# Dots, residual adds and tokens in another order: a transformer layer with 16,384 retrieved experts

## The reference, cut to what matters

```
x = LayerNorm(alpha * x + concat(diff_attention, stick_attention) @ w_out)      # "LN1"
q = x @ w_q                         # 8 heads, two halves of 128 each
s1, s2 = q . subkeys                # two times 128 scores a head
top 16 of s1, top 16 of s2, top 16 of the 256 sums  ->  16 experts a head, gates = softmax
act = gelu(x . peer_u[expert]) * gate
y = LayerNorm(alpha * x + sum act * peer_v[expert])                             # "LN2"
```

## Time and profile before

| | us |
|---|---|
| median of 3 runs | 2603.69 (2603.02 to 2605.6) |
| the profiled execution | 2600.89 |
| its span, first to last instruction | 2599.2 |
| PE busy | 2306.4 (89%) |
| DVE busy | 1468.4 (56%) |
| POOL busy | 678.5 (26%) |
| ACT busy | 377.4 (15%) |
| DMA 41%, PE 34%, DVE 14% | shares of the chain that ended last |

### The profile page before, as it was taken

One profiled execution on the slowest core, in us unless ns is written; L12 is line 12 of the kernel. 1 busy time (PEld: TensorE's weight loads), 2 busy tenths in 40 slices (PEclk: granted clock), 3 DMA queues, 4 the chain that ended last, 5 costly groups with the idle time before them and its releaser, 6 DMA issues.

```text
span 2599.2 us, 29221 instructions
## 1 busy us (share of the span) xinstructions
PE 2306.4 (89%) x11802; PEld 1677.5 (65%) x11802; DVE 1468.4 (56%) x2342; ACT 377.4 (15%) x657; POOL 678.5 (26%) x470
## 2 busy tenths in 40 slices
PE   8999999988965498887497999999999999999990
PEld 8999999947622388886487999644444444444440
DVE  3333333353578978776785760255555555555568
ACT  3333333321000211000032320000000000000001
POOL 2000000000254534221401010143334443443452
PEclk9999999999987699999799999999999999999995
DMA  6434444365999799999989988999999999999994
GB/s 251 142 141 145 141 141 144 144 262 219 405 391 397 295 421 376 417 421 421 396 290 365 361 320 318 343 415 413 418 418 418 408 421 414 417 416 420 417 394 200
DMA packets 129924, 861.41 MB, mean 331 GB/s; under 512 B 14752, under 2 KB 14880, under 8 KB 33824
## 3 DMA queue, kind: packets, MB, share of 16 engines
q1 hardware_dynamic: 63360, 425.88, 41.9%
q0 software_dynamic: 56960, 408.97, 38.7%
q10 hardware_dynamic: 9504, 25.17, 2.5%
HBM read 833.75 MB, written 26.21 MB: 331 GB/s over the span
## 4 chain that ended last, share of the span: by engine, by line
DMA 41%; PE 34%; DVE 14%; issue 5%; POOL 4%; ACT 1%; DVEq 0%; SPq 0%; ACTq 0%; POOLq 0%
DMA scratch<-peer_v,idx_v 26%; DMA arena<-peer_u,idx_u 13%; PE bank L1250 9%; DVE scratch L1642 5%; PE bank L970 4%; PE bank L971 3%; PE bank L974 3%; PE bank L1233 3%; POOL arena L576 2%; PE bank L1092 2%; DVE arena L1581 2%; PE bank L992 2%; PE bank L988 2%; PE bank L989 2%; DMA cache<-u_tiles 2%
## 5 line engine op out<-in xcount | busy, mean ns | idle before, releaser
L1581 DVE CUSTOM_DVE_ANT_0 arena<-arena,x 128x2048 f32<-128x2048 f32 x256 | 583.1, 2287 | 171.5 <-DMA arena<-peer_u,idx_u 171.2
L576 POOL DMA_INDIRECT arena<-peer_u,idx_u x256 | 358.0, 1398 | 650.2 <-DVE dots L1581 601.6
L1642 DVE SCALAR_TENSOR_TENSOR scratch<-scratch,gate 128x2048 f32<-128x2048 f32 x112 | 263.3, 2351 | 378.7 <-DMA scratch<-peer_v,idx_v 378.0
L591 POOL DMA_INDIRECT scratch<-peer_v,idx_v x112 | 251.8, 2249 | 462.9 <-DVE scratch L1642 444.7
L1250 PE MATMUL bank<-scratch,cache 128*128 128x128 f32 x2048 | 242.3, 278 | 40.1 <-DMA cache<-u_tiles 40.1
L1293 DVE TENSOR_TENSOR arena_rounded<-arena,w_high 128x1024 fp32r<-128x1024 f32 x96 | 113.9, 1224 | 266.5 <-ACT w_high L658 266.5
L1250 PEld LDWEIGHTS bank<-scratch,cache 128*128 128x128 f32 x2048 | 235.8, 194 | 44.4 <-DMA cache<-u_tiles 44.4
L1250 PE MATMUL bank<-scratch,ln_rows 128*128 128x128 f32 x2048 | 239.1, 276 | 26.2 <-DMA ln_rows<-u_tiles 22.6
L1250 PEld LDWEIGHTS bank<-scratch,ln_rows 128*128 128x128 f32 x2048 | 232.6, 192 | 30.5 <-DMA ln_rows<-u_tiles 28.4
L1270 PE MATMUL bank<-ln_rows,scratch 128*128 128x512 f32 x512 | 230.3, 592 | 0.7 <-ACT scratch L837 0.7
L1270 PE MATMUL bank<-cache,scratch 128*128 128x512 f32 x512 | 230.2, 592 | 0.0
(11 more groups left out here) (209 smaller groups left out, 2843.4 us busy)
## 6 DMA issues: line engine op xcount, KB each, us to landing
ln_rows<-u_tiles SPq DMA_DIRECT2D x64, 1024.0 KB, 8.9
cache<-u_tiles SPq DMA_DIRECT2D x64, 1024.0 KB, 10.0
ln_rows<-peer_v SPq DMA_DIRECT2D x64, 1024.0 KB, 10.0
cache<-peer_v SPq DMA_DIRECT2D x64, 1024.0 KB, 9.1
arena<-w_heads SPq DMA_DIRECT2D x32, 1024.0 KB, 5.0
arena<-w_out SPq DMA_DIRECT2D x24, 1024.0 KB, 8.3
arena<-w_heads SPq DMA_DIRECT2D x8, 2048.0 KB, 8.6
arena<-w_q SPq DMA_DIRECT2D x16, 1024.0 KB, 9.0
```

The source lines that it names most:

```text
L576: pool.indirect_dma_start(out=u_row[k % U_SLOTS], out_offset=None, in_=peer_u, in_offset=bass.IndirectOffsetOnAxis(ap=idx_u[:, p % 2, k:k ...
L591: pool.indirect_dma_start(out=v_row[slot], out_offset=None, in_=peer_v, in_offset=bass.IndirectOffsetOnAxis(ap=idx_v[:, q % 2, k:k + 1], a ...
L1581: dve.tensor_tensor_reduce(u_row[slot], u_row[slot], x1[:, 0 if p < H else 2, :], 1.0, 0.0, ALU.mult, ALU.add, dots[:, p % 2, k:k + 1]).th ...
L1642: dve.scalar_tensor_tensor(out=residual2, in0=v_row[slot], scalar=coef[:, GROUPS_DENSE + q, k:k + 1], in1=residual2, op0=ALU.mult, op1=ALU ...
```

## The change

- `add_residual(1, 0..3)` and LN1 of blocks 1 and 2 stand among 2, 2, 3, 3, 2, 2, 2 dots of group 1, instead of behind groups 1 and 2 and most of 3. `dots_and_choice(2, 0, 2)` and group 3 follow LN1.
- The choices of blocks 1 and 2 take groups 5, 6, 7; the last, `choose(1, 3)`, has no dots in it, and an explicit `weigh(7)` follows. Group 8, the first of block 2, moves into the tokens.
- Tokens begin at tiles 70 and 94 instead of 54 and 78. One dot stands ahead of every 16 tokens and six between, as before: they are dots 128 to 149 instead of 144 to 165.
- `TOGETHER` is 176 instead of 168: the dots left after the tokens are 150 to 175 (26) instead of 166 and 167; 80 instead of 88 dots remain for the second half.
- Key scores of block 0 get buffers of their own for pieces 1 and 2, so `copy_keys` waits only for piece 3. ACT's list is reordered to match: `copies(3)` ahead of the second exponents, LN1's scaling ahead of gelu 1, the third exponents and gelu 2 and 3 among the queries, gelu 8 and 9 in or after the tokens.

```diff
-TOGETHER = H * K + 40
+TOGETHER = H * K + 48
-HOT_AT = (54, 78)
+HOT_AT = (70, 94)
...
-        key_scores = [[cache[:, 3, :].rearrange("p (c l k) -> p c l k", c=2, l=LANES)] * 4,
-                      [flat[:, 3 * ROW + j * 1024:3 * ROW + (j + 1) * 1024]
-                       .rearrange("p (c l k) -> p c l k", c=2, l=LANES) for j in range(4)]]
+        after = [flat[:, 3 * ROW + j * 1024:3 * ROW + (j + 1) * 1024].rearrange("p (c l k) -> p c l k", c=2, l=LANES)
+                 for j in range(6)]
+        old_keys = cache[:, 3, :].rearrange("p (c l k) -> p c l k", c=2, l=LANES)
+        key_scores = [[old_keys, after[0], after[1], old_keys], after[2:6]]
...
# ACT
-                if grp == 0:
-                    act.wait_ge(half_read[grp], j + LEAD)
+                if grp == 0 and j == 3:
+                    act.wait_ge(half_read[grp], 1 + LEAD)
...
-            for i in range(2):
-                copy_query(0, 3, i)
+            copies(3)
             gate_numerators(0, 1)
...
             activate(0)
-            activate(1)
-            for i in range(2):
-                copy_keys(0, 3, i)
-            gate_numerators(0, 2)
-            activate(2)
             ln1_deviation(1)
             ln1_scale(1)
             copy_x1T(1)
+            activate(1)
...
-            activate(3)
...
+            gate_numerators(0, 2)
             queries(0)
+            activate(2)
             queries(1)
+            activate(3)
+            queries(2)
+            queries(3)
             gate_numerators(0, 3)
             activate(4)
-            queries(2)
-            queries(3)
-            dense = 0
-            for j, upto in enumerate((2, 6, 10, HOT_AT[0] // A_CHUNK)):
+            for c in range(4):
+                activate_dense(c)
+            dense = 4
+            for j, upto in enumerate((8, 12, 15, HOT_AT[0] // A_CHUNK)):
                 gate_numerators(1, j)
-                activate(5 + j)
+                if j < 3:
+                    activate(5 + j)
...
+                if t == HOT_AT[1] + P // HOT_PER_TILE + 4:
+                    activate(H + 1)
...
-                            activate(TOGETHER // K - 1)
+                            activate(H)
...
-            active = TOGETHER // K
+            active = H + 2
...
# DVE
-                if k == 3 and p > 0:
+                if k == 3 and p not in (0, H):
                     weigh(p - 1)
...
             dots_and_choice(0, 0, 1)
-            dots_of(1, 0, 8)
+            dots_of(1, 0, 2)
             add_residual(1, 0, out_banks(0), 4)
-            dots_of(1, 8, 16)
+            dots_of(1, 2, 4)
             add_residual(1, 1, out_banks(1), 2 * 4)
-            dots_and_choice(2, 0, 2)
+            dots_of(1, 4, 7)
             add_residual(1, 2, out_banks(2), 3 * 4)
+            dots_of(1, 7, 10)
             add_residual(1, 3, out_banks(3), 4 * 4)
             ln1_moments(1)
-            dots_of(3, 0, 2)
+            dots_of(1, 10, 12)
             ln1_shift(1)
-            dots_of(3, 2, 6)
+            dots_of(1, 12, 14)
             ln1_affine(1, 0)
-            dots_of(3, 6, 10)
             ln1_affine(1, 1)
-            dots_of(3, 10, 16)
+            dots_of(1, 14, 16)
+            dots_and_choice(2, 0, 2)
+            dots_of(3)
             dots_and_choice(4, 0, 3)
-            for j in range(4):
+            for j in range(3):
                 dots_and_choice(5 + j, 1, j)
-            i = (H + 1) * K
+            choose(1, 3)
+            weigh(H - 1)
+            i = H * K
```

## The result

The change makes the kernel faster, by less than half of what was forecast: 2588.8 us (median of four runs, 2587.9 to 2591.0) against 2604.6 us for the kernel before (median of four), ratio 0.9936 [0.9925, 0.9948]. That is 15.8 us less, where 34.9 were forecast (2569 us); 2588.8 lies in the range given. The profiled execution has a span of 2586.9 us, 12.3 less than before.

A forecast was written before the change was run, and what follows sets the result against it. No single bound: PE, DMA or DVE by stretch, so load time in the holes was counted. 10.8 (first token) + 13.8 (after the tokens) + 10.3 (second pass) = 34.9 us off 2603.7 gave 2569 us, range 2548 to 2594.

The forecast's parts named there:

- LN1 among few dots: First residual adds and LN1: LN1 ends at 821 instead of 887.8 us, DMA losing some load time before 801 and 821.
- Queries: Query columns before the first tile: PE waits some 18 us for ACT; first tile at 972 against 1011.3, 39 us earlier.
- Choices: Expert choices: choose(0,3) ends at 986, three more at 1254, the lone one takes 29 us; first token 1295, 10.8 us earlier.
- Tokens: 256 tokens with 22 dots: same work 16 tiles later, 227 us from first token to last dot, ending at 1522.
- After the tokens: 26 dots before the second pass use DMA's unused share; it starts at 1631, 24.6 us earlier, 14 of them new here.
- F: Rival, 0.02: loads after the tokens run at 377 GB/s instead of 421, costing 12 us more; 2581 us.
- Second pass: Up to the last add: about four fewer gathers of u to land, 10.3 us less; bounds 0 and 20.6.
- C: Rival, 0.14: the second pass gives nothing, as an add waits for its slot, not for bytes; 2579 us.
- E: Rival, 0.08: queries are not held, first tile at 953; only half of the 19 us is kept; 2559 us.
- D: Rival, 0.10: DVE comes late to tile 70 after a long lone choice; the hole partly stays; 2583 us.
- B: Rival, 0.08, slower: ACT's list holds the queries, dots beside w_q run at 4.97, first token 32 us later; 2611 us.

The follow-up runs named there:

- tiles-held run: Changed kernel with the loads of expert tiles 2 and on held until the last dot of group 4; ratio 0.9951 to the kernel before.
- the run without the eight dots: Changed kernel with TOGETHER back at 168, so 18 instead of 26 dots after the tokens; ratio 0.9901 to the kernel before.
- gelu 3 later: Changed kernel with ACT's gelu of group 3 moved behind the query copies of column three; ratio 0.9986 to the kernel before.

## Why the prediction was wrong

The sign was right and the size was not: 15.8 us by the medians and 12.3 in the profiled execution, not 34.9. The step that failed is `choose(0,3)` with its dots: the prediction let it run at DVE's pace, 51.2 us, and it took 68.1, at the pace of loads shared with the tiles.

- **LN1 among few dots**: right to the microsecond (821 forecast, 820.9). Its price in loads, the ten us before 821 and some before 801, was too low: 25 us unused in that stage against 6 before.
- **Queries**: PE waits for gelu 3 as forecast, and longer (28.6 us, not 18). From 823 to 946 the loads ran at 387 GB/s, not 421, and moved 387 x 123 = 47.6 MB, 45.4 MiB, not 43. Dots are 11 us late (945.4 instead of 934), the first tile 9.
- **Choices: the step that failed.** "`choose(0,3)` with group 4 is DVE-bound [...] so 986": it ended at 1013.5. DVE was busy 51.02 us in it, the forecast's 51.2, but the stretch took 68.1. Starting at 945 it runs beside tiles from 981 on, and there six dots took 32.5 us, the last ones 4.97 apart and each waiting for its gather (the two dots in the timeline above). The tiles-held run gives 11 of the 17 us to the tiles' share of the loads; even there the choice took 56.9 us, and what makes the 6 us above DVE's work was not followed. The prediction's own row had warned: beside w_q the same choice took 65.8 us for 51.24 of DVE's work. The next three choices took 271.5 us for 268 forecast, the lone one 28 to 31 for 29. With the 11 us above this brings the first token to 1322.9 instead of 1295: 17 us later than before where 10.8 earlier was forecast.
- **Tokens**: 225.5 us to the last one for 227. Right.
- **After the tokens**: 114.6 us for 109 (1631 - 1522), with PE waiting 30.75 us, as described. The 22.5 us of unused load time found there are the change's real gain ahead of the second pass; the forecast's 14 us were right in kind and 8 in size (122.8 - 114.6). The loads held 404 GB/s there, which is not F's 377, and 414 over the 881 us that follow. The Trainium skill's figure ("DMA: Bandwidth & Descriptors", "Where 436 GB/s comes from"), about 358 between HBM and SBUF, does not agree, and the measurement decides.
- **Second pass**: 19.7 us instead of 10.3, near the upper bound. What the DMA queues moved from its start to the last add, first before, then after (packets, MB, share; q0 carries the gathers, q1 what SP loads, q10 what ACT loads):

```profile
q0 software_dynamic: 30528, 222.31, 59.3%
q1 hardware_dynamic: 22517, 141.35, 38.2%
q10 hardware_dynamic: 4464, 8.13, 2.4%
...
q0 software_dynamic: 29756, 216.64, 59.2%
q1 hardware_dynamic: 22320, 139.99, 38.6%
q10 hardware_dynamic: 4320, 7.87, 2.4%
```

The gathers are 5.7 MB less, 5.4 gathers (212 to 206.6) and not four. The tiles and gates are 1.6 MB less, a term that the prediction put at nothing: what SP had issued by the start had all landed after PE's long wait, while before 1.3 MiB of it were still to come. At 411 GB/s these 7.3 MB are 17.7 us; the other 2 are a slightly higher rate, 411.4 GB/s instead of 410.6.

In the sum: the first token came 17.1 us later instead of 10.8 earlier, the second pass started 7.4 later instead of 24.6 earlier, and took 19.7 less instead of 10.3. Of the rivals, C is refuted (the second pass gave more, not nothing). E (queries not held) was built, and is slower instead of faster. D and B had the right place, DVE late to tile 70. D's reason, a long lone choice, was not it (28 to 31 us for 29); B's was near, dots slowed by other loads, but beside tiles and much less beside w_q (dot 63 ended at 945, not 972). B's 32 us at the first token were 17, and the second pass kept the sign. That the time lies in the range all the same is in part luck: the second pass gave 9.4 us more than its term, and hid a third of what was lost at the first token (28 us against the forecast). The mistake under these steps is one of bookkeeping: I priced LN1's order by where LN1 and the first tile end, and let the dots that it leaves undone come back at DVE's pace. They come back at the loads' pace, against the tiles.

What stays open: why the run without the eight dots has its first token 6.1 us earlier, and the 6 us of the third choice with the tiles held.

## What to carry to other kernels

Where one resource bounds most of a program, make the account by stage in its unused time, before and after, and price a moved step by what it fills or leaves empty there; an engine's earlier milestone is worth nothing unless the end waits for it. A step that frees the loads early isn't free if the work it displaces has to share them later with transfers that nobody needs yet. Look for the stage with the most unused time (here the tokens, 50 us) and put the displaced work there.

## What the runs showed of the hardware

Two kinds of loads in flight shared the rate about evenly here, whichever was needed first. With the tiles running, 19 tiles and 16 dots took 88.9 us at 421 GB/s in the run with gelu 3 later, although the dots were late and the tiles early; of the runs made, only the one that holds the tiles changed that. It let a choice of 51 us of DVE's work end in 56.9 us instead of 68.1. And sixteen more gathers and dots in the tokens took 9.5 us for 36.6 us of DVE work, with the clock at 0.96 and PE's busy time up from 206.6 to 216.9: about three quarters of DVE's work was covered.
